# Four levels of a triangular inverse on one core: two pieces of the next pair's projections issued ahead of the growth products in place of behind them

## The reference, cut to what matters

```
def step(s, inp):
    r_t, w_t, k_t, v_t, a_t, b_t = inp
    sa = jnp.einsum('bhvk,bhk->bhv', s, a_t)
    s = s * w_t[:, :, None, :] + sa[..., None] * b_t[:, :, None, :] + v_t[..., None] * k_t[:, :, None, :]
    return s, jnp.einsum('bhvk,bhk->bhv', s, r_t)
```

## Time and profile before

| | |
|---|---|
| median of three runs | 3219.71 us (3218.81 to 3226.44) |
| profiled execution, its time | 3223.59 us |
| profiled execution, its span | 3221.8 us |
| TensorE busy | 2775.2 us, 86% |
| VectorE busy | 1062.2 us, 33% |
| ScalarE busy | 676.9 us, 21% |
| GpSimd busy | 355.4 us, 11% |
| mean TensorE clock granted | 0.921 of full |
| the 16 pairs | from about 276 to 1310 us of the span, 65.07 us a pair in the middle (line 722 starts a pair at 623.83 us and the next at 688.90 us) |

### The profile page before, as it was taken

One profiled execution on the slowest core, in us unless ns is written; L12 is line 12 of the kernel. 1 busy time (PEld: TensorE's weight loads), 2 busy tenths in 40 slices (PEclk: granted clock), 3 DMA queues, 4 the chain that ended last, 5 costly groups with the idle time before them and its releaser, 6 DMA issues. The chain is left out here.

```text
span 3221.8 us, 68715 instructions
## 1 busy us (share of the span) xinstructions
PE 2775.2 (86%) x29670; PEld 1863.8 (58%) x29670; DVE 1062.2 (33%) x2333; ACT 676.9 (21%) x1391; POOL 355.4 (11%) x358
## 2 busy tenths in 40 slices
PE   4537999999999999858999859989889995988797
PEld 0014877787777777634877644434544442564586
DVE  0143445444544454233432510003631112114511
ACT  0023334333433333001001020001431103001511
POOL 0002333333333333000000000000000000000000
PEclk7568999999999999867999889999999997999898
DMA  9802111111111110311432212211022211230142
GB/s 328 327 14 68 34 42 39 31 39 38 44 31 39 38 44 3 106 55 72 151 111 84 79 53 100 76 66 58 1 79 74 78 62 52 99 136 26 65 149 94
DMA packets 68018, 248.36 MB, mean 77 GB/s; under 512 B 10119, under 2 KB 15848, under 8 KB 66280
## 3 DMA queue, kind: packets, MB, share of 16 engines
q1 hardware_dynamic: 66024, 240.19, 22.0%
q10 hardware_dynamic: 1728, 4.20, 0.3%
HBM read 243.32 MB, written 1.05 MB: 76 GB/s over the span
## 5 line engine op out<-in xcount | busy, mean ns | idle before, releaser
L121 PE MATMUL ps<-h,ring 128*128 128x256 f32 (+1 forms) x2048 | 593.7, 453 | 61.6 <-DMA ring<-in_w_feature 43.2
L121 PEld LDWEIGHTS ps<-h,ring 128*128 128x128 f32 x2048 | 395.7, 194 | 260.1 <-issue 190.5
L2162 PE MATMUL ps<-h,ring 128*128 128x512 f32 (+1 forms) x768 | 261.1, 494 | 17.3 <-DMA ring<-in_w_merge 17.3
L2162 PEld LDWEIGHTS ps<-h,ring 128*128 128x128 f32 x768 | 148.5, 194 | 120.9 <-issue 92.6
L1744 PE MATMUL ps<-ring,h 128*128 128x512 f32 x352 | 157.9, 604 | 21.3 <-DMA ring<-in_w_token 21.3
L132 DVE COPY features<-ps 128x512 f32 (+2 forms) x64 | 37.9, 592 | 359.6 <-PE ps L121 359.6
L282 PE MATMUL ps<-ring,cond 128*4 128x512 f32 x384 | 82.6, 1006 | 80.7 <-DMA ring<-in_w_mods 77.6
L585 PE MATMUL ps<-ring,mix_v 128*128 128x128 f32 x1024 | 150.5, 284 | 0.4 <-DVE coef L1249 0.3
L2169 PE MATMUL ps<-features,ring 128*128 128x512 f32 (+1 forms) x384 | 135.8, 500 | 9.5 <-DVE features L2128 9.5
L567 PE MATMUL ps<-mix_k,ring 128*128 128x512 f32 x256 | 136.2, 619 | 0.9 <-ACT h L932 0.9
L1005 ACT ACTIVATE U<-ps 128x256 f32<-128x256 f32 (+1 forms) x192 | 80.9, 421 | 248.6 <-PE ps L722 247.7
(11 more groups left out here) (298 smaller groups left out, 4183.3 us busy)
## 6 DMA issues: line engine op xcount, KB each, us to landing
ring<-in_w_mods SPq DMA_DIRECT2D x96, 512.0 KB, 6.2
ring<-in_w_merge SPq DMA_DIRECT2D x48, 768.0 KB, 4.2
ring<-in_w_rkvg SPq DMA_DIRECT2D x64, 512.0 KB, 3.8
ring<-in_w_feature SPq DMA_DIRECT2D x64, 512.0 KB, 3.7
ring<-in_w_in SPq DMA_DIRECT2D x48, 512.0 KB, 3.5
ring<-in_w_out SPq DMA_DIRECT2D x32, 512.0 KB, 4.8
ring<-in_w_token SPq DMA_DIRECT2D x6, 2048.0 KB, 9.2
ring<-in_w_gate SPq DMA_DIRECT2D x16, 512.0 KB, 4.9
```

Source lines behind the costliest of these rows:

```text
L121: mm = pe.matmul(R.ps[:, j % 4, 0:N], R.ring[:, j * S + k // 8, a:a + P], rhs(k), start=(k == 0), stop=(k == K - 1))
L2162: mm = pe.matmul(R.ps[:, 2 * b, 0:NQ], wt[:, b, k, :], R.h[:, k, 0:NQ], start=(k == 0), stop=(k == KD - 1))
```

## The change

At levels 1 to 4 the two calls of `next(part, None)` that stood behind the two calls of `grow` now stand ahead of them. Level 5 is as before. No instruction is added or removed, and VectorE, ScalarE, GpSimd and the DMA queue keep their order.

```diff
@@ -875,10 +875,14 @@
                 turn_inverse(1)
                 next(part, None)
             next(part, None)
+            if l < LAST:
+                next(part, None)
+                next(part, None)
             grow(i, 0, l)
             grow(i, 1, l)
-            next(part, None)
-            next(part, None)
+            if l == LAST:
+                next(part, None)
+                next(part, None)
         for z in range(2):
             pe.wait_ge(t_out[z], LAST * (i + 1))
             seen_values(i, z)
```

## The result

The changed kernel takes 3259.86 us (median of 4 runs, 3254.21 to 3262.12), the kernel before 3220.57 us beside it. The ratio is 1.0116, with a 95% interval of 1.0097 to 1.0135. By the ratio that is 37 us more (the two medians differ by 39), where 18.5 were forecast.

The account below looks back on a forecast made before the run. TensorE's queue was taken to bound the kernel. 14.6 us for pairs 2 to 15, 0.4 for the first and 3.5 for the last made 18.5 us, 3238 us against the median of 3219.7; range 3228 to 3251.

Parts of the forecast that it names:

- Line 585's wait: At level 3, line 585 right behind line 644 waits for VectorE's copy: 0.42 us more in pairs 2 to 15.
- Growth to products: Where the growth touches the next level's products, start to start takes 1.27 us, costing 0.20 to 0.31 us a level.
- The levels: Costs per pair at levels 1 to 4: 0.11, 0.31, 0.63 and -0.01 us, together 1.04 us.
- so I add nothing for them: Behind the growth, products of z = 0 take about the 0.47 us that z = 1's sums need; no added cost.
- a middle pair should take 66.1 us and not 65.07: Sign to look for in the changed profile: the length of a pair in the middle of the program.
- Waits costed at nothing: Waits at level 1's key transposes, level 2's reads and the DMA queue were taken to add no time.
- The third set of key transposes: At level 1 it waits for ScalarE's copy until 1.34 us, due at 1.36; a miss costs under 0.05 us a pair.
- The last pair: No projections stand between its transposes: 2.1 us at levels 1 and 2, and 1.4 us for the clock, 3.5 us.
- The clock term: In the last pair, more gaps may bring the fall to 0.50 forward by up to 5 us; 1.4 us taken.
- The DMA queue's waits are for the ends of the projections, which move by under 1 us: Transfers have a whole pair of 65 us, so these waits were costed at nothing.
- The third rival: Growth and products together with a gap lower the clock in each pair: 3254 us, or 3302 for all four growths; chance 0.06.
- The faster rival: TensorE changes mode less often at each level of pairs 2 to 15: 12.6 us gained, 3207 us; chance 0.03.

Follow-up runs that it names:

- the wait alone: The kernel before with one TensorE wait added: level 3's growth waits for VectorE's copy of what line 644 made; 3243.86 us, ratio 1.0058.
- run 3: Not a run label: in "then run 3 to 7 us at half clock" it is a verb and a time, so no kernel or measurement belongs to it.
- levels 1, 2 and 4: The changed kernel with level 3 put back as before, so the move is made at three levels only; 3235.55 us, ratio 1.0034.
- the other bank: The changed kernel with line 644 writing to PSUM bank 5, not 1, so line 585 need not wait for VectorE's copy; 3236.82 us, ratio 1.0046.
- the move at level 2: The kernel before with level 2's key projection piece moved from ahead of level 3's products to behind them; 3220.03 us, ratio 0.9988.
- the weights later: The changed kernel with the next key weights fetched only after VectorE's floor at level 5; 3249.78 us, ratio 1.0075.

## Why the prediction was wrong

- *Direction: right; steady cost: near.* Line 585's wait was to cost 0.42 us, and the wait alone measured 0.42 (64.55 to 64.97). Growth to products came out at 1.27 to 1.28 us as forecast.
- *The levels.* Forecast 0.11, 0.31, 0.63 and -0.01, in sum 1.04; from starts in the changed trace against those of before they are 0.10, 0.34, 0.60 and 0.01, and 0.17 more at level 5, in sum 1.22. The term that was too small is "so I add nothing for them" on the products of z = 1: at level 5 the products of z = 0 are half as long and no longer cover VectorE's second pair of sums. 14 pairs, 2.4 us. The sign "a middle pair should take 66.1 us and not 65.07" took a disturbed pair for the base; a steady one went from 64.55 to 65.77.
- *Waits costed at nothing.* The third set of key transposes fitted: 635.01 + 0.86 = 635.87, its start in the row, no idle time.
- *The last pair.* Forecast 3.5 us; from its start at line 710 to the stage's output transposes it takes 54.3 us and not 52.8, 1.5 us more. The clock term had the wrong sign: some 12 us of it were at half clock and not 17 to 18. Against that stands a stop of 1.6 us at line 737 where the kernel before has one of 0.36.
- *What was missing, and put the time out of the range: 21 us.* The step that failed is "The DMA queue's waits are for the ends of the projections, which move by under 1 us": it took the transfers of weights for the only ones that matter and put the cost at nothing. TensorE's instructions come by DMA too. A wait right behind line 644 holds the queue for 0.4 us at the point where the next key weights are asked for; the block that used to start ahead of them starts 3.3 to 4.4 us behind line 644, and four pairs of the changed kernel stand still for 1.7 to 2.5 us and then run 3 to 7 us at half clock, 4 to 6.5 us each.
- *The third rival* had a loss through the clock, and a clock of 0.50 is in the trace. As a cause it is wrong: three of the four falls come within a stop and one 0.3 us behind it, and gaps of 0.2 us behind the growth never brought it about: in the runs of levels 1, 2 and 4 and of the other bank the granted clock is 1.00 in every 10 us from 300 to 1260 us.
- *The faster rival* was wrong about this kernel, and the seams it rests on are real: they pay for level 4, and for the 0.31 us of the move at level 2.

What stays open: the trace shows when a block of instructions starts and ends and not when it is asked for. That the wait makes the block late is shown by adding it alone and by taking it away; that it does so because the held queue asks late is the reading that fits, and no run shows why 0.42 us of wait should move a block by 2 to 4 us where no weights are in transfer. That the stop is want of instructions rests on its place inside a group without waits, at the same record in four kernels, and on the 1.2 to 1.6 us from the block's end to going on in all 74 stops. In pairs 5 and 9 both kernels have no block between 3.1 us ahead of line 644 and 3.5 us behind it, and no stop: the place of the block in the program counts too.

## What to carry to other kernels

Where an in-order queue has no idle time, a piece behind a product is worth the other engines' answer it hides (at level 4 0.21 us and not its own 1.5), so before moving it read the distance between product and next user at a place where nothing stands between. Do not price a new wait by its length alone: 14 waits of 0.42 us cost three times their own sum here, because what was delayed with them was the engine's own code. To find such a thing, look for idle time that the profile gives no releaser inside a group without waits, and ask the DMA view for the instruction queue around it: here the packet ended 1.2 to 1.6 us ahead of going on every time. And check in the timeline that a piece that is moved is not an empty one.

## What the runs showed of the hardware

- TensorE stopped for 1.5 to 3.0 us at places fixed by the instruction and not by the time: the same records of line 737 in four kernels that reach the fourth of them at 1053 to 1064 us.
- Each of 74 stops of 0.4 to 3.0 us that the profile puts down to "issue", in twelve traces, ended 1.2 to 1.6 us after the end of the latest 16 KB packet of instructions.
- One added wait of 0.42 us a pair, with the order and the number of records unchanged, took 3243.86 us and not 3224.43, and in the pair of the 2.97 us stop the packet started 4.3 us behind line 644, where in the same pair of the kernel before one starts 2.4 us ahead.
- A stop of 1.9 us or more in the changed kernel was followed by 6.8 us at a granted clock of 0.50, the one of 1.7 us by 3.4 us, and those of up to 1.5 us by none. The length of the stop does not fix this: with the wait alone one of 2.25 us was followed by none, and with the weights later one of 0.84 us by 3.4 us.
- In each of the 14 pairs of the changed kernel that fetch key weights beside line 644 a packet of instructions started 3.2 to 4.6 us behind line 644, close to the weights' landing, and none earlier while they were in transfer.
